# Five gate projections of an attention block as seven half-size products each, with two weight sums of four on GpSimd and two on VectorE

## The reference

```
h    = rmsnorm(x, norm_g) * (1 + scale) + shift
proj = h @ w_in                                   # [256, 1024] @ [1024, 8192]
qkv, z_attn, u_pool, z_pool, g_attn, g_pool = split(proj, ...)   # 4608, 512, 512, 512, 1024, 1024
for g in 3 groups:                                # 8 heads of 64 each
    logits = q k^T * 64**-0.5 + bias, masked      # o_g, lse_g
wts  = softmax(stack(lse), axis=0)
attn = sum(wts * o)                               # one softmax over the keys of all three groups
y_attn = (attn * silu(z_attn)) @ w_attn_br
y_pool = (pool(u_pool) @ pool_w * pool_scale * silu(z_pool)) @ w_pool_br
merged = sigmoid(g_attn) * y_attn + sigmoid(g_pool) * y_pool
x = rmsnorm(x + gate * (merged @ w_out), final_g)
```

## Time and profile before

| | us |
|---|---|
| median of 3 runs | 1729.51 (1729.23 to 1729.88) |
| the profiled execution's own time | 1729.43 |
| its span | 1727.6 |
| attention stretch, 1566.20 to 1666.10 of the span | 99.90 |
| TensorE, VectorE, ScalarE, GpSimd busy in it | 98.62, 62.03, 23.84, 1.29 |
| half-size products before it, 1462.46 to 1566.20 | 103.74 |
| branch products, 1666.10 to 1693.80 | 27.70 |

### The profile page before, as it was taken

One profiled execution on the slowest core, in us unless ns is written; L12 is line 12 of the kernel. 1 busy time (PEld: TensorE's weight loads), 2 busy tenths in 40 slices (PEclk: granted clock), 3 DMA queues, 4 the chain that ended last, 5 costly groups with the idle time before them and its releaser, 6 DMA issues.

```text
span 1727.6 us, 24448 instructions
## 1 busy us (share of the span) xinstructions
PE 1701.1 (98%) x10237; PEld 1000.9 (58%) x10237; DVE 582.6 (34%) x1085; ACT 264.8 (15%) x455; POOL 26.2 (2%) x37
## 2 busy tenths in 40 slices
PE   9999999999999999999999999999999999999998
PEld 8787888888643433333333343433333338998885
DVE  4684368454341111111111111112121135545643
ACT  1323115002011111101011010101010121112211
POOL 1000000100000000000000000000000000000000
PEclk9999999999999999999999999999999999999999
DMA  9564332545979999999999999999999996443241
GB/s 343 193 257 162 146 123 100 173 162 204 365 308 427 406 427 429 426 427 429 428 429 428 428 429 427 429 427 429 427 429 426 429 413 251 189 154 147 98 142 48
DMA packets 61970, 540.52 MB, mean 313 GB/s; under 512 B 5193, under 2 KB 12137, under 8 KB 32453
## 3 DMA queue, kind: packets, MB, share of 16 engines
q1 hardware_dynamic: 56160, 528.42, 74.4%
q10 hardware_dynamic: 3956, 5.86, 1.2%
q0 software_dynamic: 1776, 5.10, 0.9%
HBM read 533.57 MB, written 5.78 MB: 312 GB/s over the span
## 4 chain that ended last, share of the span: by engine, by line
PE 93%; DMA 3%; DVE 2%; ACT 1%; issue 1%; SPq 0%; DVEq 0%; ACTq 0%
PE small L1487 24%; PE small L1526 13%; PE proj L859 10%; PE proj L1680 7%; PE proj L1043 5%; PE proj L1759 4%; PE proj L1463 3%; PE small L1429 3%; PE small L1475 2%; PE small L1494 2%; PE small L1122 2%; PE small L879 2%; PE proj L868 2%; PE small L1626 2%; PE small L1819 2%; PE small L1353 2%
## 5 line engine op out<-in xcount | busy, mean ns | idle before, releaser
L1487 PE MATMUL small<-arena 128*64 128x512 f32 x2048 | 446.2, 593 | 2.5 <-DMA arena<-in_expert_w_gu 1.2
L1487 PEld LDWEIGHTS small<-arena 128*64 128x64 f32 x2048 | 151.3, 137 | 281.6 <-issue 275.7
L1526 PE MATMUL small<-arena 128*64 128x512 f32 x1024 | 227.0, 595 | 8.1 <-ACT arena L2015 7.3
L2703 DVE TENSOR_SCALAR arena<-small 128x512 f32<-128x512 f32 x32 | 22.1, 692 | 533.7 <-PE small L1494 533.7
L859 PE MATMUL proj<-arena 128*128 128x256 f32 x832 | 182.9, 380 | 0.0
L859 PEld LDWEIGHTS proj<-arena 128*128 128x128 f32 x832 | 157.2, 190 | 21.9 <-issue 0.5
L1526 PEld LDWEIGHTS small<-arena 128*64 128x64 f32 x1024 | 74.2, 137 | 139.4 <-issue 138.4
L1680 PE MATMUL proj<-arena 128*128 128x128 f32 x1120 | 125.7, 275 | 0.5 <-ACT arena L2092 0.5
L1680 PEld LDWEIGHTS proj<-arena 128*128 128x128 f32 x1120 | 125.3, 192 | 0.7 <-ACT arena L2092 0.7
L2010 ACT ACTIVATE arena<-arena 128x512 f32<-128x512 f32 x32 | 20.1, 629 | 490.5 <-DVE arena L2703 490.5
L1840 ACT ACTIVATE arena<-proj 128x512 f32<-128x512 f32 (+2 forms) x72 | 41.5, 592 | 329.2 <-PE proj L859 128.9
(11 more groups left out here) (454 smaller groups left out, 1540.3 us busy)
## 6 DMA issues: line engine op xcount, KB each, us to landing
arena<-in_expert_w_gu SPq DMA_DIRECT2D x128, 2048.0 KB, 19.2
arena<-in_expert_w_down SPq DMA_DIRECT2D x47, 2048.0 KB, 27.1
arena<-in_w_in_first SPq DMA_DIRECT2D x20, 2048.0 KB, 8.7
arena<-in_w_in SPq DMA_DIRECT2D x15, 2048.0 KB, 7.4
arena<-in_expert_w_down SPq DMA_DIRECT2D x17, 1536.0 KB, 29.2
arena<-in_w_ada SPq DMA_DIRECT2D x6, 2048.0 KB, 12.4
arena<-in_expert_w_down SPq DMA_DIRECT2D x17, 512.0 KB, 30.7
arena<-in_w_branch SPq DMA_DIRECT2D x4, 2048.0 KB, 8.1
```

Of the source, the lines that this page charges most:

```text
L1487: mm = pe.matmul(bank[CAP * half:CAP * half + CAP, :], XG[:, k % 4, k // 4, :], w[:, k % 4, n * D + half * W:n * D + half * W + W], start= ...
L1526: mm = pe.matmul(bank[CAP * half:CAP * half + CAP, :], h[:, m, u, :], w[:, half * W:half * W + W], start=u == 0 and m == 0, stop=u == 1 an ...
```

## The change

ZP and the four gate units join `SPLIT`, so that 35 products take the place of the ten fills; `FILLS` is gone. `ENDS` is now the place of U, and `LATER` are the five new units. Their products, sums, copies and adds are written out by hand between the pieces of the attention in the programs of TensorE, ScalarE and VectorE.

- GpSimd makes T1 = B12 - B11 and T2 = B22 - T1 of a new unit, VectorE T3 = B22 - B12 and T4 = B21 - T2.
- The new units have one running bank and one bank for P2 and P7; the scores have the other two (`score_bank`), so a block of scores waits until the one before is out.
- Two rooms of the ring hold the gates' weights in turn, the third (that of Z) the sums T1 and T2; the load of a unit waits for the last product (P4) of the unit two before. `Wb2p` is loaded after the last product of g2p 1.
- The token sums S1 to S4 lie in another place, since the gates' tile is written earlier.
- The sigmoids of the pool's gate run as two passes over what the adds have left, not on the way out of PSUM.
- The first three pieces of the attention branch go ahead of the pool's matmul; the pooling on VectorE goes behind the attention's last product; the first block of scores goes into the last unit of the stage before.

```diff
-FILLS = ["ZP 0", "ZP 1"] + [f"g2{b} {i}" for b in "ap" for i in range(4)]
+GATES2 = ["ZP", "g2a 0", "g2a 1", "g2p 0", "g2p 1"]
-        SPLIT = QKV_RUN[1:] + ["Z", "U"]
+        SPLIT = QKV_RUN[1:] + ["Z", "U"] + GATES2
+        HOMES = {"ZP": "ZP", "g2a 0": "U", "g2a 1": "ZP", "g2p 0": "U", "g2p 1": "ZP",
+                 "Wb2a": "U", "Wb2p": "Z", "out2 0": "ZP", "out2 1": "U"}
...
# GpSimd
+            pool.wait_ge(sig("split_weights"), 4 * (ENDS + 1))
+            for u in LATER:
+                n = unit2_no(SPLIT[u])
+                pool.wait_ge(sig("split_full"), multiplied("P4", ENDS - 1 if u == LATER[0] else u - 2))
+                pool.wait_ge(sig(f"unit2_in_{n % 3}"), 16 * (n // 3 + (n % 3 > 0)))
+                w = split_weights(u)
+                pool.wait_ge(sig("split_weights"), 4 * u)
+                pool.tensor_tensor(w["T1"], w["B12"], w["B11"], ALU.subtract).then_inc(sig("split_weights"), 1)
+                pool.wait_ge(sig("split_weights"), 4 * u + 1)
+                pool.tensor_tensor(w["T2"], w["B22"], w["T1"], ALU.subtract).then_inc(sig("split_weights"), 1)
...
# TensorE
+            def gate_6(u):
+                pe.wait_ge(sig("split_weights"), 4 * u + 2)
+                pe.wait_ge(sig("split_copied"), copied_out("C11", u))
+                split_product(u, "U", "S2", "T2", False)
+            def gate_7(u):
+                pe.wait_ge(sig("split_weights"), 4 * u + 3)
+                pe.wait_ge(sig("split_added"), added_up("C11", u))
+                split_product(u, "P7", "S3", "T3", True)
...
+            def gate_4(u):
+                pe.wait_ge(sig("split_weights"), 4 * u + 4)
+                pe.wait_ge(sig("split_added"), added_up("C22", u))
+                split_product(u, "P7", "A22", "T4", False)
...
+            gate_1(zp_); gate_2(zp_); scores(0, 1); gate_6(zp_); gate_7(zp_); gate_5(zp_)
+            scores(0, 2); gate_3(zp_); gate_4(zp_)
+            scores(1, 0); gate_1(a0); gate_2(a0); scores(1, 1); gate_6(a0); gate_7(a0); weights_turned(0)
+            gate_5(a0); scores(1, 2); gate_3(a0); weights_turned(1); gate_4(a0); gate_1(a1); weighted(0)
+            scores(2, 0); gate_2(a1); gate_6(a1); scores(2, 1); gate_7(a1); gate_5(a1); weights_turned(2)
+            gate_3(a1); scores(2, 2); gate_4(a1); weights_turned(3); gate_1(p0); gate_2(p0); weighted(1)
+            scores(3, 0); gate_6(p0); scores(3, 1); gate_7(p0); gate_5(p0); scores(3, 2); gate_3(p0)
+            weights_turned(4); gate_4(p0); weights_turned(5); gate_1(p1); gate_2(p1); weighted(2)
+            weights_turned(6); gate_6(p1); weights_turned(7); gate_7(p1); gate_5(p1); weighted(3)
+            gate_3(p1); gate_4(p1)
...
# VectorE
+            biased(0, 0); c21(ENDS); gate_sums(zp_); c11(zp_); biased(0, 1); c22(zp_)
+            biased(0, 2); maxima(0, 0); maxima(0, 1); c21(zp_); biased(1, 0); gate_sums(a0)
+            scaled(0); c11(a0); scaled(1); biased(1, 1); turned_copied(0); c22(a0)
+            biased(1, 2); maxima(1, 0); turned_copied(1); c21(a0); maxima(1, 1); scaled(2); gate_sums(a1)
+            gated(0); biased(2, 0); c11(a1); scaled(3); biased(2, 1); c22(a1); turned_copied(2)
+            biased(2, 2); maxima(2, 0); c21(a1); turned_copied(3); gate_sums(p0); maxima(2, 1)
+            c11(p0); scaled(4); gated(1); biased(3, 0); scaled(5); biased(3, 1); c22(p0)
+            biased(3, 2); maxima(3, 0); turned_copied(4); c21(p0); maxima(3, 1); gate_sums(p1); turned_copied(5)
+            c11(p1); scaled(6); gated(2); scaled(7); turned_copied(6); turned_copied(7); c22(p1); gated(3)
```

More of the change, by code:

```diff
@@ L1707, in split_unit @@
                     product_1(u + 1)
+                else:
+                    for _ in range(2):
+                        pe.nop().then_inc(sig("proj_full"), 1)
+                    scores(0, 0)
                 pe.wait_ge(sig("split_copied"), copied_out("C22", u))
@@ L1779, in weighted @@
                 mm.then_inc(sig("small_full"), 1)
[L1781 to L1801, removed]
+            zp_, a0, a1, p0, p1 = LATER
@@ new lines, in _ @@
+            gate_1(zp_)
+            gate_2(zp_)
+            scores(0, 1)
+            gate_6(zp_)
+            gate_7(zp_)
+            gate_5(zp_)
+            scores(0, 2)
+            gate_3(zp_)
+            gate_4(zp_)
+            scores(1, 0)
+            gate_1(a0)
+            gate_2(a0)
+            scores(1, 1)
+            gate_6(a0)
+            gate_7(a0)
+            weights_turned(0)
+            gate_5(a0)
+            scores(1, 2)
+            gate_3(a0)
+            weights_turned(1)
@@ new lines, in _ @@
+            gate_4(a0)
+            gate_1(a1)
+            weighted(0)
+            scores(2, 0)
+            gate_2(a1)
+            gate_6(a1)
+            scores(2, 1)
+            gate_7(a1)
+            gate_5(a1)
+            weights_turned(2)
+            gate_3(a1)
+            scores(2, 2)
+            gate_4(a1)
+            weights_turned(3)
+            gate_1(p0)
+            gate_2(p0)
+            weighted(1)
+            scores(3, 0)
+            gate_6(p0)
+            scores(3, 1)
@@ L1802, in _ @@
+            gate_7(p0)
+            gate_5(p0)
+            scores(3, 2)
+            gate_3(p0)
+            weights_turned(4)
+            gate_4(p0)
+            weights_turned(5)
+            gate_1(p1)
+            gate_2(p1)
+            weighted(2)
+            weights_turned(6)
+            gate_6(p1)
+            weights_turned(7)
+            gate_7(p1)
+            gate_5(p1)
+            weighted(3)
+            gate_3(p1)
+            gate_4(p1)
             pe.wait_ge(sig("attn_done"), 1)
+            merge2("Wb2a", attn, range(3))
@@ L2119, in _ @@
-            fill(0)
+            zp_, a0, a1, p0, p1 = LATER
+            split_copy(zp_, "P1", 0, 0)
+            split_copy(zp_, "P6", 1, 0)
+            split_copy(zp_, "P5", 1, 1)
+            split_copy(zp_, "P3", 0, 1)
             exponentials(0)
             exponentials(1)
[L2122 to L2127, removed]
+            split_copy(a0, "P1", 0, 0)
@@ L2821, in _ @@
             ada(5)
-            for u in range(len(SPLIT)):
+            for u in range(ENDS + 1):
                 if u:
@@ L2833, in _ @@
                 else:
[L2834 to L2849, removed]
-                        do(TTn(PB[h % 4][:, lo:lo + w_].rearrange("p (g c) -> p g c", c=n),
-                               proj_bank[m % 4][:, 0:w_].rearrange("p (g c) -> p g c", c=n), bias, ALU.add), "proj_out")
@@ L2885, in _ @@
[L2885 to L2893 removed]
+            biased(1, 1)
+            turned_copied(0)
+            c22(a0)
+            biased(1, 2)
+            maxima(1, 0)
+            turned_copied(1)
+            c21(a0)
+            maxima(1, 1)
@@ new lines, in _ @@
+            scaled(2)
+            gate_sums(a1)
+            gated(0)
+            biased(2, 0)
+            c11(a1)
+            scaled(3)
+            biased(2, 1)
+            c22(a1)
+            turned_copied(2)
+            biased(2, 2)
+            maxima(2, 0)
+            c21(a1)
+            turned_copied(3)
+            gate_sums(p0)
+            maxima(2, 1)
+            c11(p0)
+            scaled(4)
+            gated(1)
+            biased(3, 0)
+            scaled(5)
+            biased(3, 1)
@@ L2894, in _ @@
+            c22(p0)
+            biased(3, 2)
+            maxima(3, 0)
+            turned_copied(4)
+            c21(p0)
+            maxima(3, 1)
+            gate_sums(p1)
+            turned_copied(5)
+            c11(p1)
+            scaled(6)
+            gated(2)
+            scaled(7)
             turned_copied(6)
             turned_copied(7)
+            c22(p1)
+            gated(3)
+            dve.wait_ge(sig("zsig"), 1)
+            do(TTn(attn, attn, zsig, ALU.mult), "attn_done")
```

263 lines of the change are left out of this document (171 added, 92 removed).

## The result

The changed kernel took 1735.08 us (median of 8 runs, 1732.30 to 1737.72) against 1729.45 before (1728.92 to 1729.88): ratio 1.0032, interval 1.0023 to 1.0042. The change makes the kernel slower by 0.3%, where 1729.1 us and a range up to 1732.6 were forecast.

What follows compares the result with a forecast made beforehand. TensorE was taken to bound the attention stretch. -7.74 (products for fills) - 2.17 (gaps) + 5.15 (stalls) = -4.76, then + 0.72 + 3.71 (scalings waiting) = -0.33 us, so 1729.1 us; range 1723.8 to 1732.6.

Steps and rivals of the forecast that it cites:

- its open question: Attention stretch: whether VectorE's scalings wait beside GpSimd's passes, which no row prices; forecast as waiting, 0.72 and 3.71 us.
- Products for fills, -7.74 us: TensorE, attention stretch: ten fills (70.29 us) go and 35 products at 1.787 us (62.55) come, 7.74 us less.
- old gaps, -2.17: TensorE, attention stretch: six idle gaps, of 0.19 to 0.57 us, go with the change, 2.17 us in all.
- That the products might not run at 1.787 us among the scores I count small.: Attention stretch: products between scores and turned heads keep their 1.787 us, since such pieces already stood between fills without gaps.
- VectorE's order, stalls of 0.68, 0, 2.09 and 2.38 us: TensorE waits for VectorE's fixed order in g2a 0, g2a 1, g2p 0 and g2p 1: 5.15 us in all.
- above 80 us busy: Sign that the forecast is right: VectorE's busy time in the attention stretch, from 62 to some 81 us.
- The scalings' wait, 0.72 + 3.71: VectorE waits until GpSimd's passes end: 0.72 us at g2a 1 (head 1), 3.71 at g2p 1 (maximum's scaling, head 4).
- The passes interleave: Rival: GpSimd's second pass gets between head 1's two scalings, costing 3.02 us in place of 0.72; 1731.4 us, chance 0.22.
- The sum, which takes TensorE's work behind a stall at its usual price: Adding up the terms for the attention stretch: each stall costs its length only, with nothing added for TensorE's work after it.
- Every add with an addend in memory waits as well.: Rival: VectorE's adds beside GpSimd passes wait too, at four places, 14.6 us on top of 1724.7; 1739.3 us, chance 0.10.
- the rule it cites on the shared ports: Skill text: a VectorE two-port or two-SBUF-input instruction and a GpSimd one exclude each other; the first keeps the ports throughout.
- this forecast or the third case below: The two outcomes said to follow from the cited port rule: VectorE waiting (1729.1 us), or a case not named further.

Runs made afterwards that it cites:

- the first experiment: Changed kernel with GpSimd's passes for g2a 1, g2p 0 and g2p 1 waiting until heads 1, 3 and 5 are scaled: 1726.49 us, 0.9987 of the kernel before.

## Why the prediction was wrong

The forecast was a gain of 0.3 us and a range up to 1732.6; measured was a loss of 5.6. Two terms that the prediction put at nothing failed: TensorE's clock behind a stall, and the price of a product that stands beside scores. The waits for GpSimd, its open question, came out near their forecast. By its own steps:

- *Products for fills, -7.74 us; old gaps, -2.17.* Right as a count; not the whole price. In the first experiment's kernel the stretch from 1561.35 to 1661.29 is 99.94 us, 2.92 less than before. -7.74 - 2.17 + 4.27 of its gaps leave 2.7 us unaccounted for.
- *"That the products might not run at 1.787 us among the scores I count small."* This step failed: it is where those 2.7 us are. In that kernel, from start to next start and without gaps, the 35 new products come to 65.2 us and not 62.55; the scores' 0.7 more and the turned heads' 0.7 less cancel. A product between two turned heads takes 1.79 (1637.08 to 1638.87), one between scores and a turned head 1.89 (1634.21 to 1636.10):

```profile
1634.21 2.05 PE L1740 MATMUL proj<-arena 128*128 128x128 f32 x16
1636.10 1.15 PE L1800 MATMUL small<-arena 128*128 128x128 f32 x9
1637.08 1.95 PE L1740 MATMUL proj<-arena 128*128 128x128 f32 x16
1638.87 1.15 PE L1800 MATMUL small<-arena 128*128 128x128 f32 x9
```

Two products between two blocks of scores take 3.77 (1629.57 to 1633.34) for 3.57 in a run. So about 0.1 us is paid at each change from products to scores or a weighted pair, and at each change back from scores. I looked only for gaps, and none shows. Why a change costs this no run tells. The fills paid the same tenth (half a fill 3.45 before turned heads, 3.55 before a weighted pair), but ten fills have fewer such changes than seven products a unit, spread between the pieces.

- *VectorE's order, stalls of 0.68, 0, 2.09 and 2.38 us.* Held: 0.17, 0, 1.78 and 2.32 where GpSimd is out of the way. The walk by durations and queue order found each place. The sign "above 80 us busy" came true by luck: 83.1 here holds 9.6 us of waiting, and without the waits it is 73.5, since the pooling left the stretch.
- *The scalings' wait, 0.72 + 3.71.* That scalings wait was right, at heads 1 and 4 as said, and at head 3, where it cost no gap. How they wait was the rival's way (*"The passes interleave"*): both scalings of a head wait, a pass each. At head 4 the forecast had the small scaling of a maximum wait and then one pass more; in the trace that scaling is through (1627.43 to 1627.60) before the pass of 1627.97, and the two scalings bring 3.78. That this is so near to 3.71 is luck. The gaps come to 10.01 for 4.27 without the meetings: 5.74 us; the forecast had 4.43, the interleaved case 6.73.
- *"The passes interleave" (1731.4)* is what happened to VectorE and TensorE's gaps. With TensorE kept busy in its gaps the kernel takes 1732.62, at the very end of the range.
- *The sum, which takes TensorE's work behind a stall at its usual price.* This is the other step that failed. The forecast put a stall of 5.80 us before the second scores block of pair 3 (5.57 measured), but gave nothing for what comes after. The half clock added 0.53 on the scores, 2.54 on two products and 1.66 on the weighted pair: 4.73 us in the profiled run. At the median it is 2.5 (1735.08 against 1732.62 with the gaps filled). Without this term the time lies at the end of the range (1732.62); without the 2.7 us of the changes it would have been just inside (1732.4, an estimate). The Trainium skill, "TensorE: Matmul & The Clock Gate", section "Part 1: The HAM clock gate", says that an idle TensorE is put to 1.2 GHz and comes back only after being busy for a while. The traces agree (0.50 behind gaps of 5.57, 4.43 and 2.31 us), and I had not weighed it.
- *"Every add with an addend in memory waits as well."* Refuted by the bias adds and C11 beside a pass. Where the prediction says that the rule it cites on the shared ports leads to "this forecast or the third case below", the case meant can only be the interleaving: the rule as cited wants two inputs in memory, and these adds have one. For a scaling (2.45 us for 0.63) and for a sum with two inputs in memory (3.18 for 1.225) the runs bear that rule out.

Account of the profiled run, +8.29 us: -7.74 - 2.17 + 10.01 of gaps + 4.73 of clock + 2.7 at the changes = 7.5; 0.3 is a later start of the stretch, 0.3 lies outside the span (1737.72 - 1735.6, before 1729.43 - 1727.6), and 0.2 is not assigned.

## What to carry to other kernels

Work that goes to GpSimd must be placed in time as well as on an engine: have it wait until VectorE's scalings and sums with two inputs in memory are through, if it has time to spare. Price a TensorE stall twice, for its length and for the half clock that can follow it; if it cannot be removed, matmuls without use keep the rest at speed. Take the price of a piece from a row where it stands between the same neighbours, not from a long run of its kind. Weight sums with a late need belong behind the bias adds and copies that TensorE waits for.

## What the runs showed of the hardware

- A VectorE instruction that waits for a GpSimd pass shows it as a longer duration (2.45 us for 0.63), not as idle time before it, and the reverse (2.55 for 2.35). The two engines take turns, so a chain of two scalings pays for two passes (4.86 us for 1.08).
- Scalings (2.45 us for 0.63) and sums with two inputs in memory (3.18 for 1.225) wait; adds with one input in PSUM do not (1.52 us for a pair of bias adds, 0.42 for C11).
- A gap of 2.32 us lowered the clock in one profile and not in another, and gaps of 2.10, 2.31 and 2.33 did in the one profile each was in; so a kernel can have two groups of times 1.7 us apart. The gaps of 4.29, 4.43, 4.84 and 5.57 did each in the one profile that shows it.
- In float32, a change between products of 128x128 weights and scores or weighted pairs, with weights half that size, costs about 0.1 us without a gap (1.89 us for 1.79).
